# A two-layer hybrid decoder trunk on one core: another order of its first loads and first units, room for two slots' raw weights, and products of zeros ahead of the first transposes

## What is computed

```
h = rms_norm(x, pre_g);  u = h @ W_in            # 1024 -> 2560, ten blocks of 256 columns
A: conv      a * sigmoid(gate), causal depthwise conv of width 31, LayerNorm, swish
B: retention 4 heads of 64, rotary, chunks of 128, GroupNorm, swish gate
C: MoBA      4 heads of 64, blocks of 256, softmax over past and own block
D: pool      causal means over 2, 4, 8, 16 tokens, minus the token, per-group map
x = x + rms_norm(concat(A, B, C, D) @ W_out, post_g)
h = rms_norm(x, fpre_g);  x = x + rms_norm((silu(h @ W_gate) * (h @ W_up)) @ W_down, fpost_g)
```

## Time and profile before

| | before |
|---|---|
| median of three runs | 1109.45 us |
| the profiled execution's own time | 1109.05 us |
| its span, first to last instruction | 1107.2 us |
| TensorE busy (matmuls) | 1079.1 us, 97% |
| VectorE busy | 620.5 us, 56% |
| ScalarE busy | 410.3 us, 37% |
| GpSimd busy | 5.1 us |
| read from HBM | 106.46 MB |

### The profile page before, as it was taken

One profiled execution on the slowest core, in us unless ns is written; L12 is line 12 of the kernel. 1 busy time (PEld: TensorE's weight loads), 2 busy tenths in 40 slices (PEclk: granted clock), 3 DMA queues, 4 the chain that ended last, 5 costly groups with the idle time before them and its releaser, 6 DMA issues.

```text
span 1107.2 us, 16624 instructions
## 1 busy us (share of the span) xinstructions
PE 1079.1 (97%) x6640; PEld 656.5 (59%) x6640; DVE 620.5 (56%) x1418; ACT 410.3 (37%) x810; POOL 5.1 (0%) x18
## 2 busy tenths in 40 slices
PE   5999999999999999999999999999999999999997
PEld 4888785596444444444478878747844444444443
DVE  5898998884324324312568989889624324322014
ACT  4454635454323323212234463455523323322001
POOL 1000000000000000000000000000000000000000
PEclk9999999999999999999999999999999999999999
DMA  7442403155234233233003341034533333232001
GB/s 272 132 131 77 154 1 115 39 177 164 80 113 149 80 114 112 95 99 114 1 1 115 115 135 57 1 114 135 176 110 110 101 113 111 81 113 76 1 20 57
DMA packets 58172, 109.64 MB, mean 99 GB/s; under 512 B 7024, under 2 KB 7280, under 8 KB 57968
## 3 DMA queue, kind: packets, MB, share of 16 engines
q1 hardware_dynamic: 58096, 108.58, 31.1%
HBM read 106.46 MB, written 2.10 MB: 98 GB/s over the span
## 4 chain that ended last, share of the span: by engine, by line
PE 88%; DVE 6%; DMA 4%; issue 1%; ACT 1%; SPq 0%; ACTq 0%; DVEq 0%
PE ps L493 82%; DMA raw<-weights_dram 3%; PE ps L497 3%; DVE ring L1134 2%; DVE E L1255 2%; PE ps L696 1%; PE ps L680 1%; DMA gbc<-gains_dram 1%; DVE E L1207 0%; ACT ring L758 0%; DVE small L1437 0%; DVE hT L1215 0%; ACT gbc L758 0%; DVE U L1358 0%; PE ps L657 0%
## 5 line engine op out<-in xcount | busy, mean ns | idle before, releaser
L493 PE MATMUL ps<-hT,ring 128*128 128x512 f16 (+1 forms) x3264 | 549.0, 330 | 2.8 <-DVE hT L1215 2.7
L493 PEld LDWEIGHTS ps<-hT,ring 128*128 128x128 f16 x3264 | 320.4, 98 | 226.6 <-issue 3.1
L493 PE MATMUL ps<-ring,U 128*128 128x512 f16 x1440 | 313.4, 379 | 0.0
L1134 DVE SCALAR_TENSOR_TENSOR ring<-raw,ring 128x512 f16<-128x512 f32 x376 | 236.8, 685 | 97.5 <-ACT ring L758 96.7
L758 ACT ACTIVATE ring<-raw 128x512 f16<-128x512 f32 x376 | 212.9, 622 | 140.3 <-PE ps L493 81.2
L493 PEld LDWEIGHTS ps<-ring,U 128*128 128x128 f16 x1440 | 140.8, 98 | 167.1 <-issue 0.3
L1458 DVE SCALAR_TENSOR_TENSOR R<-ps,R 128x512 f32<-128x512 f32 (+1 forms) x52 | 31.7, 609 | 255.4 <-ACT R L933 255.0
L493 PE MATMUL ps<-ring,hT 128*128 128x256 f16 x1152 | 134.3, 273 | 0.0
L933 ACT ACTIVATE R<-ps 128x512 f32<-128x512 f32 (+1 forms) x52 | 27.5, 530 | 275.4 <-PE ps L493 275.4
L493 PEld LDWEIGHTS ps<-ring,hT 128*128 128x128 f16 x1152 | 112.2, 98 | 14.2 <-issue 1.1
L1255 DVE SCALAR_TENSOR_TENSOR E<-E,par 128x256 f32<-128x256 f32 x240 | 101.7, 477 | 0.2
(11 more groups left out here) (104 smaller groups left out, 475.7 us busy)
## 6 DMA issues: line engine op xcount, KB each, us to landing
raw<-weights_dram SPq DMA_DIRECT2D x376, 256.0 KB, 3.4
gbc<-gains_dram SPq DMA_DIRECT2D x8, 512.0 KB, 6.1
xs<-x_dram SPq DMA_DIRECT2D x4, 512.0 KB, 5.3
out_dram<-xs SPq DMA_DIRECT2D x8, 256.0 KB, 2.0
cst<-consts_dram SPq DMA_DIRECT2D x1, 1296.0 KB, 8.2
bd<-pool_w_dram SPq DMA_DIRECT2D x8, 16.0 KB, 5.6
par<-params_dram SPq DMA_DIRECT2D x1, 76.0 KB, 6.0
cst<-consts_dram SPq DMA_DIRECT2D x1, 64.0 KB, 5.8
```

Of the source, the lines that this page charges most:

```text
L493: ins = mm(dst, st, mv_, start=first and i == 0, stop=last and i == 2, **kw)
L1134: V.scalar_tensor_tensor(out=ring[:, slot % RING, 1, raw_part(part)], in0=raw[:, n % NRAW, :], scalar=W_SCALE, in1=ring[:, slot % RING, 0, ...
```

## The change

- The gain's and the identity's loads are issued ahead of x tile 1.
- The order of the W_in slots is MQ, MK, CONV_A, CONV_G | MV, RQ, RK, RV | POOL, RG.
- The raw parts 4 to 11 (slots 1 and 2) have room of their own in ycat, the buffer of the mixers' outputs, which is empty until the mixers end; SP issues their loads without a wait. Parts 12 on use the four raw buffers as before.
- In layer 0, unit 0 waits for the low splits of slot 0 part by part (a part holds two of the eight k) and, as in every unit of slot 0, for h_lo of tile c only when half c begins. VectorE does the low split of part 0, then h_lo 0, then parts 1 to 3, then h_lo 1.
- VectorE first sets buffer gt (128 x 512 float32, read as float16) to zero; TensorE runs 18 products of it with itself (128 x 512) into PSUM bank 7 ahead of the wait for the identity, and 4 more between the transposes of tiles 0 and 1.
- AT and both engines' sequences are written anew for both layers. In the loop over layers VectorE does norm_x 2 ahead of the last norm_y of the layer before, takes up slots 4 to 6, MoBA's first rotation and the GLU before the first conv taps; low splits of slots 9 to 14 and the mixers' steps are moved against each other, `zero` (two memsets) comes behind slot 10. At the end of a layer norm_y 2 goes ahead of h_lo 0 and 1.

```diff
-CONV_A, CONV_G, MQ, MK, MV, RQ, RK, RV, POOL, RG = range(10)
+MQ, MK, CONV_A, CONV_G, MV, RQ, RK, RV, POOL, RG = range(10)
...
 AT = [
     {
-        ("pre_T", 2): 55, ("pre_T", 3): 57, ("moba_T", 0): 101, ("moba_T", 1): 115, ("moba_stage", 0): 121,
+        ("pre_T", 2): 57, ("pre_T", 3): 58, ("moba_T", 0): 96, ("moba_T", 1): 107, ("moba_stage", 0): 124,
...
-        ("conv_T", 0): 199, ("moba_stage", 6): 217, ("moba_stage", 7): 224, ("ret_T", 0): 226,
+        ("moba_stage", 6): 184, ("conv_T", 0): 186, ("moba_stage", 7): 208, ("ret_T", 0): 211,
...
-        ("fpre_T", 0): 371, ("fpre_T", 1): 376, ("fpre_T", 2): 433, ("fpre_T", 3): 436, ("pre_T", 0): 948,
-        ("pre_T", 1): 970,
+        ("fpre_T", 0): 372, ("fpre_T", 1): 374, ("fpre_T", 2): 415, ("fpre_T", 3): 438, ("pre_T", 0): 955,
+        ("pre_T", 1): 965,
     },
     {
-        ("pre_T", 2): 35, ("pre_T", 3): 46, ("moba_T", 0): 90, ("moba_T", 1): 113, ("moba_stage", 0): 117,
+        ("pre_T", 2): 0, ("pre_T", 3): 31, ("moba_T", 0): 65, ("moba_T", 1): 82, ("moba_stage", 0): 106,
...
+        def raw_home(n):
+
+            if PARTS <= n < PARTS + EARLY:
+                e = n - PARTS
+                return ycat_w[:, raw_part(e)], early_in[e], 16
+            m = n if n < PARTS else n - EARLY
+            return raw[:, m % NRAW, :], raw_in[m % NRAW], 16 * (m // NRAW + 1)
...
-            for t in range(2):
-                sp.dma_start(xs[:, t, :], x[tok(t), :]).then_inc(x_in[t], 16)
+            sp.dma_start(xs[:, 0, :], x[tok(0), :]).then_inc(x_in[0], 16)
             gain_load(1, 0)
             sp.dma_start(ident, consts[:, 0:P]).then_inc(ident_in, 16)
+            sp.dma_start(xs[:, 1, :], x[tok(1), :]).then_inc(x_in[1], 16)
...
-                if n >= NRAW:
+                dst, landed, _ = raw_home(n)
+                if n >= PARTS + EARLY + NRAW:
                     sp.wait_ge(lo_split, n - NRAW + 1)
-                sp.dma_start(raw[:, n % NRAW, :], weights[n, :, :]).then_inc(
-                    raw_in[n % NRAW], 16)
+                elif n >= PARTS + EARLY:
+                    sp.wait_ge(lo_split, n - EARLY - NRAW + 1)
+                sp.dma_start(dst, weights[n, :, :]).then_inc(landed, 16)
...
+                            if pre and k == 0:
+                                pe.wait_ge(h_lo, xno(pre, l, tiles[c]) + 1)
+                            if by_parts and c == 0 and k % 2 == 0:
+                                pe.wait_ge(lo_split, k // 2 + 1)
...
+            def wake(n):
+
+                for _ in range(n):
+                    mm(bank[7][:, :], zeros[:, 0:P], zeros[:, 0:S], start=True, stop=True)
+
+            pe.wait_ge(zeros_sb, 1)
+            wake(18)
             pe.wait_ge(ident_in, 16)
-            for t in (0, 1):
-                h_T("pre", 0, t)
+            h_T("pre", 0, 0)
+            wake(4)
+            h_T("pre", 0, 1)
...
+            V.memset(gt_w[:, :], 0.0).then_inc(zeros_sb, 1)
...
-            split_lo(0)
+            split_lo_part(0, 0)
             h_lo_of("pre", 0, 0)
+            for part in range(1, PARTS):
+                split_lo_part(0, part)
             h_lo_of("pre", 0, 1)
...
             for l in range(L):
+                z = l * SLOTS
+                norm_x("pre", l, 2)
                 norm_y("fpost", l - 1, 3)
-                zero(l)
-                norm_x("pre", l, 2)
                 norm_x("pre", l, 3)
+                split_lo(z + 4)
+                h_lo_of("pre", l, 2)
+                h_lo_of("pre", l, 3)
+                split_lo(z + 5)
+                moba_rotate(l, 0)
+                split_lo(z + 6)
                 glu(l, 0)
-                h_lo_of("pre", l, 2)
-                conv(l, 0, 1)
-                h_lo_of("pre", l, 3)
-                conv(l, 0, 4)
-                z = l * SLOTS
-                conv(l, 0, 6)
-                split_lo(z + 4)
-                moba_rotate(l, 0)
-                split_lo(z + 5)
-                conv(l, 0, 6)
-                split_lo(z + 6)
...
+                conv(l, 0, 10)
+                split_lo(z + 7)
+                conv(l, 0, 18)
...
+                norm_x("pre", l + 1, 1)
+                norm_y("fpost", l, 2)
                 h_lo_of("pre", l + 1, 0)
-                norm_x("pre", l + 1, 1)
                 h_lo_of("pre", l + 1, 1)
-                norm_y("fpost", l, 2)
```

More of the change, by code:

```diff
@@ L61 @@
 NRAW = 4
+EARLY = 2 * PARTS
 RING = 8
@@ L189, in trunk_program @@
         sink = sb("sink", [P, DM], BF16)
-        gt = sb("gt", [P, 2, HALF])[:, :, :]
+        gt_w = sb("gt", [P, 2 * HALF])
+        gt = gt_w[:, :].rearrange("p (c t) -> p c t", c=2)
+        zeros = gt_w[:, :].bitcast(F16)
         raw = sb("raw", [P, NRAW, RAW])
@@ L361, in trunk_program @@
         raw_in = [sem(f"raw_in{i}") for i in range(NRAW)]
+        early_in = [sem(f"early_in{i}") for i in range(EARLY)]
         def unit_no(l, slot, s):
@@ L513, in unit @@
                 between(0)
-                if FIRST_OF[slot] == i:
+                by_parts = l == 0 and i == 0
+                if FIRST_OF[slot] == i and not by_parts:
                     pe.wait_ge(lo_split, PARTS * (l * SLOTS + slot + 1))
@@ L959, in split_hi @@
                         i = PARTS * n + part
-                        act.wait_ge(raw_in[i % NRAW], 16 * (i // NRAW + 1))
-                        copy(ring[:, n % RING, 0, raw_part(part)], raw[:, i % NRAW, :], W_SCALE).then_inc(hi_split, 1)
+                        src, landed, value = raw_home(i)
+                        act.wait_ge(landed, value)
+                        copy(ring[:, n % RING, 0, raw_part(part)], src, W_SCALE).then_inc(hi_split, 1)
             square_x("pre", 0, 0)
@@ L1124, in rsqrt, with split_lo_part @@
                 return ins
+            def split_lo_part(slot, part):
+                n = PARTS * slot + part
+                dve.wait_ge(hi_split, n + 1)
+                V.scalar_tensor_tensor(out=ring[:, slot % RING, 1, raw_part(part)], in0=raw_home(n)[0],
+                                       scalar=W_SCALE, in1=ring[:, slot % RING, 0, raw_part(part)],
+                                       op0=ALU.mult, op1=ALU.subtract).then_inc(lo_split, 1)
             def split_lo(*slots):
@@ L1131, in split_lo @@
                     for part in range(PARTS):
-                        n = PARTS * slot + part
-                        dve.wait_ge(hi_split, n + 1)
-                        V.scalar_tensor_tensor(out=ring[:, slot % RING, 1, raw_part(part)], in0=raw[:, n % NRAW, :],
-                                               scalar=W_SCALE, in1=ring[:, slot % RING, 0, raw_part(part)],
-                                               op0=ALU.mult, op1=ALU.subtract).then_inc(lo_split, 1)
+                        split_lo_part(slot, part)
             def rstd(c, mean_done, other=None):
@@ L1520, in _ @@
                 m_max(l, 0, 1)
-                conv(l, 0, 9)
+                conv(l, 0, 1)
+                moba_rotate(l, 1)
                 m_max(l, 0, 2)
-                conv(l, 0, 3)
-                split_lo(z + 7)
+                conv(l, 0, 2)
+                split_lo(z + 8)
                 m_max(l, 0, 3)
-                moba_rotate(l, 1)
-                split_lo(z + 8)
-                conv(l, 0, 3)
+                conv(l, 0, 11)
                 m_max(l, 1, 0)
+                glu(l, 1)
                 conv(l, 0, 1)
                 m_max(l, 1, 1)
-                conv(l, 0, 3)
-                ret_rotate(l, 0, 0)
-                conv(l, 0, 3)
+                conv(l, 0, 7)
                 m_max(l, 1, 2)
```

179 lines of the change are left out of this document (94 added, 85 removed).

## The result

The changed kernel takes 1100.84 us (median of four, 1099.62 to 1101.61). Its ratio to the kernel before is 0.9918, interval [0.9902, 0.9933]; a second set of rounds gave 1100.80 and 0.9908 [0.9890, 0.9926]. The change is worth 9 us (8.3 between the two profiled executions), where 5.0 were forecast, and the time lies just under the range (1101.0 to 1108.0). The profiled execution took 1100.66, with a span of 1098.9 against 1107.2.

The account below looks back on a forecast made before the run. TensorE, busy 97% of the span, bounds the kernel, so time is won where it idles or runs slower, mostly the head. Head 5.0 us and mixers nothing off 1109.05 give 1104.05, plus 0.40 for the median 1104.4; range 1101.0 to 1108.0.

Parts of the forecast that it names:

- The head: Start of the kernel up to unit 4: unit 4 would start at 37.65 instead of 42.68, a gain of 5.0 us.
- The zeros: Head: products of zeros raise TensorE's clock level early, so all 192 real products run at 0.109 us; worth 2.1 to 2.7.
- level low again or never raised: Rival, head: zeros and transposes do not hold the upper clock level; gain only 2.7 us, 1106.7; chance 0.15.
- I cost the mixers' order at nothing in both layers: Mixers of layers 0 and 1: the re-ordered work was forecast to gain or lose 0 us.
- the bounds: Limits on the mixers' order: at best all 7.5 us idle gained, at worst a loss as in the slower rival.
- the new order also removes waits: Rival, mixers: VectorE's greater lead and later small products win 3 of the 7.5 us idle; 1101.4; chance 0.12.
- conv_T(0): Tightest place of layer 0's mixers: TensorE there at 89.7, VectorE's last tap at 89.0 to 89.2, half a microsecond of slack.
- the transposes at the start of layer 1: Layer 1's head: pre_T(2) at tick 0, 561.36, with norm 2 done at 560.9, in time by 0.5 us.
- The base: The profiled execution of the kernel before, 1109.05 us, from which 5.0 was taken; the median was put 0.40 above.
- Slower: Rival, layer 0's mixers: VectorE becomes the bound as slots 4, 5, 6 each wait a whole load and split; 1115.8; chance 0.05.
- absorbed: Rival, mixers: VectorE gives away idle time before slots 4 to 6, TensorE waits about 5 us; 1109; chance 0.06.

Follow-up runs that it names:

- a_nozeros: The changed kernel without its 22 products of zeros (the memset stays); 1101.35 us, ratio 0.9917.
- after_again: The changed kernel once more, with no edit, in five rounds; 1100.80 us.
- a_noearly: The changed kernel with raw parts 4 to 11 back in the four raw buffers, their loads waiting for low splits again; 1108.01 us, ratio 0.9978.
- a_noparts: The changed kernel with unit 0 waiting for all of slot 0 and slot 0's units for both tiles' h_lo at their start; 1105.15 us, ratio 0.9948.
- plan_only: The changed kernel with the old head: no zeros, old load order, four raw buffers, unit 0 not by parts; 1107.98 us, ratio 0.9967.
- a_moba0: The changed kernel with layer 0's ticks in layer 1, except pre_T(2) and (3) kept at 0 and 31; 1105.06 us, ratio 0.9950.
- a_late0: The changed kernel with layer 1's own ticks up to conv_T(0) at 172 and layer 0's for all later; 1103.12 us, ratio 0.9938.
- a_at1: The changed kernel with layer 0's table of ticks in layer 1 as well, the engines' sequences kept; 1107.36 us, ratio 0.9970.
- b_split: The kernel before with ScalarE's high splits of slots 13 and 14 behind its copies, slot 14's low split later on VectorE; 1124.74 us, ratio 1.0125.
- b_early: The kernel before with only the new order of the first loads and the room for slots 1 and 2; 1109.14 us, ratio 0.9993.
- before_again: The kernel before once more, with no edit, for a second profile; 1109.62 us.
- a_hlo2: The changed kernel with VectorE's h_lo(2) in the middle of slot 4's low splits instead of behind them; 1100.63 us, ratio 0.9913.
- a_oldend: The changed kernel with layer 0's ticks in layer 1, the old end of a layer and pre_T(2), (3) at 35, 46; 1104.09 us, ratio 0.9944.

## Why the prediction was right and wrong

**The head: right.** Norm 0 at 7.2 (measured 7.19), the second ending at 12.0 (12.3), first product 14.0 (14.17), half c = 1 at 17.05 (17.07), unit 1 at 19.65 (19.70), no hole in the transfers (385 to 410 GB/s from 10 to 22), slot 3's lo splits done at 27.6 (28.5), unit 4 at 37.65 with h_lo(2) as what it waits for (38.18). 5.0 forecast, 4.5 measured. Slot 3 came 0.9 late, and the two norms, costed at 6.3 us, took 5.6 and gave some of it back.

**The zeros: the level right, the value wrong.** "Value: 26 x 0.103 = 2.7 us ... so 2.1 to 2.7" forgot the wait that the same sum found at unit 4. With TensorE free for it at 37.4 and h_lo(2) at 37.65, a chain that is 2.1 later arrives at 39.5, and the sum itself gives 1.8. a_nozeros measured 1.78 at unit 1 but 0.77 at unit 4, since the waits on the way hold 1.0 us, where the sum had 0.25. The rival "level low again or never raised" was priced at 1106.7 by the same slip; the level does fall in the head in some executions, and the time is 1101 (after_again). So the head's gain is not 2.7 of clock and 2.3 of order: a_noearly makes the room for slots 1 and 2 worth 7.2 us of the whole and a_noparts the parts 4.3. They are not terms of a sum, since each needs the other's cover.

**"I cost the mixers' order at nothing in both layers": wrong.** This is the step that failed. The new plan wins 1.3 us in layer 0 and 2.5 in layer 1, together 3.8 of the 7.5 idle that the bounds allowed, and 4.8 against the mean of the four profiles with the old layer 1. That it is the plan and not the new head is shown: plan_only has the old head and wins 2.0 and 2.5. The waits that went are those of the two lists in the section on the result: 1.10 us before a retention product (L615) in layer 0, 1.37 for a copy of ScalarE (662.0) and 0.52 before conv_T(1) in layer 1; a new one of 0.96 came in layer 0, at stage 10.

Which part of the plan removes them is shown in part. In layer 1 its own ticks are needed: a_moba0 and a_late0 lose 3.0 us by the ticks behind conv_T(0), a_at1 another 2.4 by the late transposes of h. Whether the slot order, the sequences or the ticks win over the old plan, and what wins layer 0's 1.3, no run separates; b_split and a_at1, which take a piece of the sequences or all of them without the ticks made for them, lose more than the plan wins. The rival "the new order also removes waits" (3 us, 0.12) came close to the size. It named two causes, VectorE's greater lead and small products placed later. The lead did grow: the last tap of the first conv half ends 51.1 us behind the start of unit 4 instead of 52.1 (50.5 in plan_only, where unit 4 waits for h_lo(3), as in a_noparts). No run has the lead without the ticks, so its share stays open.

I had checked conv_T(0), where no wait came, as forecast (TensorE there at 90.49, last tap done at 89.31, forecast 89.7 and 89.2), and the transposes at the start of layer 1, in time as forecast too. The other small products, of 46 in each layer's table, I took as neutral.

**The base.** The sum was made against an execution with no fall of the clock in its layers. Its own time was 1109.05; the medians in later rounds were 1110.5 to 1111.3. That is 1 us of the 9. It fits that the old layer 1 takes 1.0 us more in the mean of its four profiles than in the first, by a wait of 1.92 for a copy (b_early, 671.0) and a fall of the clock (before_again). That the new order has fewer falls is not shown: the mean granted clock of its executions (0.996 to 0.998) is no higher than that of the kernel before, 0.998 in the median of its executions.

**"Slower" and "absorbed"** did not happen. The chain that "slower" described, VectorE late because each slot's splits wait for a whole load, was met, if at all, in one place: a_at1, where it cost one wait of 2.41 us. b_split is slower by 14 us for another reason, ScalarE's and VectorE's splits moved under the old ticks.

The Trainium skill (TensorE: Matmul & The Clock Gate, Part 1) has idleness bring the throttled state back. The traces agree: levels of 0.50 behind gaps of 3.6 us (a_noparts), 1.94 (a_hlo2) and even 1.3 (before_again).

## What to carry to other kernels

Before a term is added to the sum of a head, follow it to the point where the chains join: 1.8 us won at unit 1 were 0.8 at unit 4 and 0.55 at W_out, because the other chain (loads, norms, splits) is then the longer one. Where engines run written-out orders against each other, a new table of issue points is a change of its own with its own sign. It is measured by the distance between two fixed instructions in both traces. Make the forecast against the median, not against one good execution.

## What was not expected of the hardware

The clock fell to the lower level in the middle of a busy kernel, for 3.4 or 6.8 us at a time, behind single gaps of 1.30 us (before_again), 1.94 (a_hlo2) and 2.30 (plan_only), and in a_oldend behind two of 0.85 and 0.97. The length of the gap does not decide alone: waits of 1.92 us (b_early, at 671) and 2.41 (a_at1, at 600) passed without a fall. Nor does it happen in every execution of the same program: the first profile of the kernel before stood 1.37 us at 662 and has no fall, the second stood 1.30 us at the same place and has one. A fall costs 1.5 us (before_again, right behind it) to 2.4 us (a_noparts: 4.41 lost at unit 1 less the 2.05 of the later start). All-zero products raise the level as others do: in the kernel after the 18 of them are 0.427 us apart up to 5.7 and 0.216 from 6.0 on. The column of granted clocks reads 1.00 ahead of the first change of level, at either level; in the head only the pitch of the products told it.
